# RWKV chunk stage of a two-layer mixer network: the inverse's second operand by transposes, a new block order, and merged right-hand sides

## The reference, cut to what matters

```python
def step(state, inp):
    w_t, kk_t, kka_t, k_t, v_t, r_t = inp
    sk = jnp.einsum('dbhvk,dbhk->dbhv', state, kk_t)
    new = (state * w_t[..., None, :] - sk[..., :, None] * kka_t[..., None, :]
           + v_t[..., :, None] * k_t[..., None, :])
    y_fwd = jnp.einsum('bhvk,bhk->bhv', new[0], r_t[0])
    y_bwd = jnp.einsum('bhvk,bhk->bhv', state[1], r_t[1])
    return new, jnp.stack([y_fwd, y_bwd])
```

## Time and profile before

| | |
|---|---|
| median of 3 runs | 3633.68 us (3628.63 to 3635.43) |
| profiled execution, its own time | 3633.06 us |
| its span, first to last instruction | 3631.3 us |
| PE busy | 3480.8 us (96%) |
| DVE, ACT, POOL busy | 1845.9, 1182.9, 667.7 us |
| stage of the change, layer 0 | 711.0 to 818.5 us |
| the same stage, layer 1 | 1916.2 to 2020.9 us |

### The profile page before, as it was taken

The page is one execution under the profiler, slowest core; times in us unless marked ns, Lnnn a source line. Parts: engine busy times, 40 slices in busy tenths (PEclk is TensorE's granted clock), DMA queues, the critical chain, the costliest instruction groups (busy, mean ns, idle before and its releaser), DMA issues. The chain is left out here.

```text
span 3631.3 us, 52208 instructions
## 1 busy us (share of the span) xinstructions
PE 3480.8 (96%) x22144; PEld 2769.1 (76%) x22144; DVE 1845.9 (51%) x2604; ACT 1182.9 (33%) x1641; POOL 667.7 (18%) x460
## 2 busy tenths in 40 slices
PE   7999998989999999999898899999899999989999
PEld 6888774586888788887548788887678887768887
DVE  6777636735455567664575543345543335373332
ACT  3222333524222322223352432233442223253223
POOL 4202111131202120211014121220011211001112
PEclk9999999999999999999999999999999999999999
DMA  6565421002444355442000222323032322122331
GB/s 210 179 195 171 129 72 35 7 27 83 124 148 125 113 166 188 152 155 82 31 13 27 71 89 92 101 83 93 24 105 93 101 96 85 59 70 93 96 101 58
DMA packets 445211, 357.99 MB, mean 99 GB/s; under 512 B 15990, under 2 KB 441012, under 8 KB 444980
## 3 DMA queue, kind: packets, MB, share of 16 engines
q1 hardware_dynamic: 444980, 354.67, 31.1%
HBM read 350.43 MB, written 2.10 MB: 97 GB/s over the span
## 5 line engine op out<-in xcount | busy, mean ns | idle before, releaser
L587 DVE TENSOR_TENSOR ring_wlo<-ring_raw,ring_whi 128x2048 fp32r<-128x2048 f32 (+3 forms) x268 | 570.9, 2130 | 376.6 <-ACT ring_whi L568 346.5
L568 ACT ACTIVATE ring_whi<-ring_raw 128x2048 fp32r<-128x2048 f32 (+3 forms) x278 | 490.4, 1765 | 652.0 <-PE f_ps L1076 242.9
L1074 PE MATMUL f_ps<-act_hi,ring_whi 128*128 128x512 f32 x1280 | 502.0, 392 | 3.3 <-DVEq L1228 3.3
L1076 PE MATMUL f_ps<-act_hi,ring_wlo 128*128 128x512 f32 x1280 | 498.7, 390 | 0.0
L1075 PE MATMUL f_ps<-act_lo,ring_whi 128*128 128x512 f32 x1280 | 498.1, 389 | 0.0
L1184 POOL TENSOR_TENSOR f_glo<-f_v,f_ghi 128x512 fp32r<-128x512 f32 x88 | 238.0, 2704 | 1030.2 <-ACT f_ghi L1176 1030.2
L1074 PEld LDWEIGHTS f_ps<-act_hi,ring_whi 128*128 128x128 f32 x1280 | 240.3, 188 | 53.6 <-DVEq L1228 5.0
L1166 ACT ACTIVATE f_t<-f_ps 128x512 f32<-128x512 f32 x88 | 52.6, 598 | 695.6 <-PE f_ps L1076 648.2
L1076 PEld LDWEIGHTS f_ps<-act_hi,ring_wlo 128*128 128x128 f32 x1280 | 240.2, 188 | 50.7
L1075 PEld LDWEIGHTS f_ps<-act_lo,ring_whi 128*128 128x128 f32 x1280 | 240.4, 188 | 49.0
L1074 PE MATMUL f_ps<-f_ghi,ring_whi 128*128 128x512 f32 x704 | 277.0, 393 | 0.0
(11 more groups left out here) (598 smaller groups left out, 6014.2 us busy)
## 6 DMA issues: line engine op xcount, KB each, us to landing
ring_raw<-in_w_ff_in SPq DMA_DIRECT2D x176, 512.0 KB, 4.8
f_ada_raw<-in_w_ada SPq DMA_DIRECT2D x128, 512.0 KB, 5.3
ring_raw<-in_w_mlp SPq DMA_DIRECT2D x64, 1024.0 KB, 5.1
ring_raw<-in_w_in SPq DMA_DIRECT2D x42, 1024.0 KB, 5.1
ring_raw<-in_w_ff_out SPq DMA_DIRECT2D x32, 768.0 KB, 4.5
ring_raw<-in_w_ff_out SPq DMA_DIRECT2D x32, 640.0 KB, 4.0
ring_raw<-in_w_out SPq DMA_DIRECT2D x16, 1024.0 KB, 5.5
ada_raw<-in_w_ada SPq DMA_DIRECT2D x16, 512.0 KB, 8.5
```

Source lines behind the costliest of these rows:

```text
L568: eng.activation(self.w_hi[:, i % self.SPLIT, 0:s.nk, 0:w], self.raw[:, i % self.RAW, 0:s.nk, 0:w], ACT.Copy)\
L587: eng.tensor_tensor(self.w_lo[:, i % self.SPLIT, 0:s.nk, 0:w], self.raw[:, i % self.RAW, 0:s.nk, 0:w], self.w_hi[:, i % self.SPLIT, 0:s.nk ...
L1074: eng.matmul(out, wh, o_hi[:, a, :], start=(s.first and q == 0), stop=False)
L1076: return eng.matmul(out, wl, o_hi[:, a, :], start=False, stop=(s.last and q == s.nk - 1))
```

## The change

It replaces the second half of the inverse's arithmetic by transposes, lays blocks half a level apart, and merges some operands.

- `mirrored` and its bank M are gone. `masked` (DVE, four operations on 64 partitions) writes the masked A part of MR into `MA`, with rows by head parity; `started` (DVE) makes the first T^T, tile `T1`, from the same bank; `kept` (DVE) masks the R part into `ME`. Only `kept` frees the banks of MR. POOL's four operations for T^T are gone.
- X is gone. After `second` has updated `T1`, `inverse_turned` (TN) transposes it with four 128x128 transposes and ACT copies the result into `T0`. `first` multiplies `MB` with `T0` on all four quarters of the array into two half-filled banks, each copied by ACT with its own operation.
- The negated BT lies beside the R part in `ME`, so `moved` is one matmul of 128 columns in place of two of 64. POOL sums the two directions of NR's second part (`summed`), so `ended` has three terms in place of four.
- Within a level PE does: Z(a), TN(a+1), other results, XT(a), Z(a+1), other results, TN(a), XT(a+1). The other results are placed anew; block 1's YQ, for which the weight loads wait, moves from the second to the fourth level of blocks 2 and 3. A third count "m" holds DVE's reads of MR, NR and RW.

```diff
@@ rwkv_chunks, tensor
-            def mirrored(b):
...
+            def inverse_turned(b, lv):
+
+                if lv == 0:
+                    eng.wait_ge(t_first, b + 1)
+                else:
+                    read(eng, "XT", b, lv)
+                out = begin("TN", b, lv)
+                for d in (0, 1):
+                    for hh in (0, 1):
+                        col = (2 * d + hh) * P
+                        mm = eng.transpose(out[:, col:col + P], T1[b][:, d, hh, :, :].rearrange("p q c -> p (q c)"), k.ident)
                 mm.then_inc(pe_done, 1)
...
             def first(b, lv):
                 i = b % 2
                 eng.wait_ge(mb_done, (b // 2 * LEVELS + lv - 1) * 2 + i + 1)
+                read(eng, "TN", b, lv - 1)
+                outs = [begin("Z", b, 2 * lv + par) for par in (0, 1)]
+                for d in (0, 1):
+                    for hh in (0, 1):
+                        col = (2 * d + hh) * 64
+                        for c in (0, 1):
+                            for par in (0, 1):
+                                mm = eng.matmul(outs[par][tok(c), col:col + 64], MB[i][tok(par), (lv + b // 2) % 2, d, hh, c, :],
+                                                T0[i][tok(par), d, hh, c, :], start=True, stop=True)
+                                if d and hh and c:
+                                    mm.then_inc(pe_done, 1)
...
-                if lv < LEVELS:
-                    out = begin("X", b, lv)
...
+            cross("MR", 0)
+            cross("MR", 1)
+            for name in ("AT", "BT", "KT"):
+                turned(name, 0)
+            inverse_turned(0, 0)
+            cross("NR", 0)
+            for a in (0, 2):
+                for lv in range(1, LEVELS + 1):
+                    first(a, lv)
+                    inverse_turned(a + 1, lv - 1)
+                    if a == 0 and lv in (1, 5):
+                        cross("NR", 1 if lv == 1 else 3)
+                    elif a == 0 and lv == 2:
+                        turned("AT", 1)
+                        turned("BT", 1)
+                    elif a == 0:
+                        cross("MR", lv - 1)
+                    elif lv == 1:
+                        solved(0)
+                    elif lv == 2:
+                        moved(0)
+                    elif lv < 5:
+                        ended(lv - 3)
+                    else:
+                        turned("AT", 3)
+                        turned("BT", 3)
+                    second(a, lv)
+                    first(a + 1, lv)
+                    if a == 0 and lv in (1, 3):
+                        guess(lv // 2)
+                    elif a == 0 and lv == 2:
+                        turned("KT", 1)
+                    elif a == 0 and lv == 4:
+                        cross("NR", 2)
+                    elif a == 2 and lv == 1:
+                        solved(1)
+                    elif a == 2 and lv == 2:
+                        moved(1)
+                    elif a == 2 and lv == 3:
+                        turned("AT", 2)
+                        turned("BT", 2)
+                    elif a == 2:
+                        turned("KT", lv - 2)
+                        guess(lv - 2)
+                    if lv < LEVELS:
+                        inverse_turned(a, lv)
+                    elif a == 0:
+                        inverse_turned(2, 0)
+                    second(a + 1, lv)
@@ vector
+            def masked(b):
+
                 for par in (0, 1):
+                    made(eng, "MR", b, par)
+                    for c in (0, 1):
+                        ins = eng.tensor_tensor(MA[b][tok(par), :, :, c, :], parts(bank("MR", b, par)[tok(c), :], 0),
+                                                k.unseen[tok(c), :, 0:64].unsqueeze(2).to_broadcast([64, 2, 2, 64]), ALU.mult)
+                ins.then_inc(a_masked, 1)
+
+            def started(b):
+
                 for par in (0, 1):
+                    ins = eng.tensor_tensor(T1[b][:, :, :, par, :], parts(bank("MR", b, par)[:, :], 0),
+                                            k.pairs.unsqueeze(2).to_broadcast([P, 2, 2, 64]), ALU.mult)
+                ins.then_inc(t_masked, 1)
+                eng.wait_ge(t_masked, b + 1)
+                t = T1[b][:, :, :, :, :].rearrange("p d h n c -> p (d h n) c")
                 eng.tensor_tensor(t, over_heads(k.eye64, 8), t, ALU.subtract).then_inc(t_first, 1)
 
+            def kept(b):
+
+                for par in (0, 1):
+                    eng.tensor_tensor(ME[b][:, :, :, par, 0, :], parts(bank("MR", b, par)[:, :], 1),
+                                      k.unseen[:, :, 64:P].unsqueeze(2).to_broadcast([P, 2, 2, 64]), ALU.mult).then_inc(m_read, 1)
...
             for b in (0, 1):
+                masked(b)
+                started(b)
+                kept(b)
+            later(0)
+            for a in (0, 2):
+                for lv in range(1, LEVELS + 1):
+                    if a == 0 and lv in (3, 4):
+                        masked(lv - 1)
+                    second(a, lv)
+                    if a == 0 and lv in (1, 5):
+                        later(1 if lv == 1 else 3)
+                    elif a == 0 and lv in (3, 4):
+                        started(lv - 1)
+                        kept(lv - 1)
+                    elif a == 2 and lv == 2:
+                        moved(0)
+                    second(a + 1, lv)
+                    if a == 0 and lv == 4:
+                        later(2)
...
```

More of the change, by code:

```diff
@@ L247, in _ @@
             for d in (0, 1):
-                added(k.pairs[:, d, :], k.between[:, 0, :], k.seen[:, 1 - d, 0:64], ALU.mult)
+                added(k.pairs[:, d, :], k.between[:, 0, :], k.seen[:, d, 0:64], ALU.mult)
             fill(k.eye64, 0.0)
@@ L2190, in cross, with one @@
     def cross(name, b):
[L2191 to L2200, removed]
+        order.extend([(name, b, 0, "m"), (name, b, 1, "m")])
+    def one(name, b, i=0):
+        order.append((name, b, i, "s"))
@@ L2209, in rwkv_plan @@
[L2209 to L2215, removed]
@@ L2222, in rwkv_plan @@
+    for b in (2, 3):
+        solved(b)
+    for b in (2, 3):
+        cross("RW", b)
+        ended(b)
+    place, reads = {}, {"v": 0, "s": 0, "m": 0}
     for n, (name, b, i, reader) in enumerate(order):
@@ L2296, in cross @@
                                     mm.then_inc(pe_done, 1)
-            def mirrored(b):
[L2299 to L2305, removed]
-                                mm = eng.matmul(outs[par][tok(c), col:col + 64], feat["A"][rows, 2 * d + hh, at:at + 64],
-                                                feat["B"][rows, 2 * d + hh, at:at + 64], start=True, stop=True)
-                                if d and hh and c:
-                                    mm.then_inc(pe_done, 1)
             def turned(name, b):
@@ L2446, in _ @@
-            for b in (0, 1):
-                solved(b)
-                mirrored(b + 2)
-            for lv in range(1, LEVELS + 1):
-                first(2, lv)
-                first(3, lv)
-                if lv <= 2:
-                    moved(lv - 1)
-                elif lv < LEVELS:
-                    turned("AT", lv - 1)
-                    turned("BT", lv - 1)
-                second(2, lv)
-                second(3, lv)
-                if lv <= 2:
-                    ended(lv - 1)
-                elif lv < LEVELS:
-                    turned("KT", lv - 1)
-                    guess(lv - 1)
@@ L2472, in _, with summed @@
             ph.clear(eng)
+            def summed(b):
+                read(eng, "NR", b, 1)
+                eng.tensor_tensor(NR[b][:, 0, :, 1, :], NR[b][:, 0, :, 1, :], NR[b][:, 1, :, 1, :], ALU.add).then_inc(n_summed, 1)
             for b in (0, 2):
@@ L2502, in _ @@
                         eng.tensor_tensor(z[:, t, 1:S + 1], z[:, t, 1:S + 1], z[:, 2 + t, 1:S + 1], ALU.mult).then_inc(rk_done, 1)
+                summed(b)
+                summed(b + 1)
         @block.scalar
@@ L2601, in moved @@
+            def second(b, lv):
+                made(eng, "XT", b, lv)
+                if lv > 1:
+                    read(eng, "XT", b, lv - 1)
+                else:
+                    eng.wait_ge(t_first, b + 1)
+                t = T1[b][:, :, :, :, :].rearrange("p d h n c -> p (d h n c)")
+                eng.tensor_tensor(t, t, bank("XT", b, lv)[:, :], ALU.subtract).then_inc(v_read, 1)
             def moved(b):
```

358 lines of the change are left out of this document (176 added, 182 removed).

## The result

The changed kernel takes 3607.45 us (median of 4 runs, 3604.77 to 3610.34). The kernel before took 3632.22 on the same chip (4 runs, 3628.63 to 3635.43). The ratio is 0.9932, 95% interval 0.9915 to 0.9949: faster, by 24.8 us, 0.7%. The forecast was 3610 from 3633.68. One run of experiment e3, of 5004.38 us, is left out of all that follows, since its mean granted clock was 0.65 where the other runs have 0.99, and nothing here says why.

A forecast was written before the change was run, and what follows sets the result against it. PE's own work bounds the stage; 92.0 of sets - 15.5 + 11.8 new waits + 6.3 code stops gives 94.6, so -12.9 in layer 0, -10.1 in layer 1, together -23.0: 3610 us from 3633.68, range 3594 to 3622.

The forecast's parts named there:

- The sets, -15.5 us a stage: PE's matmul sets in one stage: X, M go, Z faster, TN added, RW and YQ trimmed; together -15.5 us.
- The new waits, 11.8: PE waiting on DVE, ACT and banks, at the stage's start and in its levels: 11.8 us of new waits.
- The code stops, 6.3: PE stops for 256-instruction code blocks needing about 3.6 us, in `ended`, the tail and during weight loads: 6.3 us.
- Rival 1: Code stops in the stage vanish through fewer instructions and waits: 12.6 us less for two layers, 3597; chance 0.13.
- The sum, 94.6 a stage: Layer 0's stage after the change: 92.0 - 15.5 + 11.8 + 6.3 = 94.6 us, from 107.5.
- rival 2: Clock falls at the thin start in both layers for some 8 us, adding 4 us each: 3618; chance 0.14.
- a clock below 1 inside the stage: Sign that would show the prediction wrong: granted clock below 1 within the changed stage.
- Rival 3: DVE's queue binds and the waits double: both layers +23.6, no difference left, 3634; chance 0.08.
- rival 4: Thin start lowers the clock and level gaps keep it at 1.2 GHz: slower, 3656; chance 0.06.
- Rival 5: The chain of dependent operations is looser than reckoned, waits half: -12, 3598; chance 0.11.
- Costed at nothing: POOL's `summed`, ACT's added copies, SP's later weight loads (about 20 us left), and `pairs`: no time charged.
- The term of -9.2 us for Z: Z goes from two array quarters to four: 20 sets from 0.93 to 0.47 us, -9.2 us a stage.

The follow-up runs named there:

- e3: Changed kernel with DVE's subtraction from the identity moved behind `kept` for block 1 and behind block 1's XT subtraction for blocks 2 and 3: 3608.31 us, ratio 0.9941.
- the repetition: The changed kernel run and profiled once more, unaltered: 3609.31 us, ratio 0.9937 to the kernel before.
- e1: Changed kernel with `moved` issued as two matmuls of 64 columns in place of one of 128: 3618.07 us, ratio 0.9965.
- e2: Changed kernel with Z's same 16 matmuls ordered by head parity, so neighbours use only two quarters of the array: 3613.33 us, ratio 0.9956.
- e9: Kernel of e8 with Z's matmuls ordered by head parity as in e2: 3603.16 us, ratio 0.9917.
- e6: Changed kernel with the two blocks of a pair side by side again, not half a level apart: 3622.76 us, ratio 0.9972.
- e8: Changed kernel with 14 unused transposes filling the start, TN(a+1) after the other results, identity subtraction late (block 3's behind `later(2)`): 3598.81 us, ratio 0.9909.

## Why the prediction came out right

**The sets, -15.5 us a stage: right.** PE's busy time fell by 12.7 (with some 1 us of slow clock in it) and 14.3, in records whose ends overlap; TN 0.58, Z 0.47 and the 2496 matmuls are as reckoned.

**The new waits, 11.8: right in the sum.** 9.0 us of idle time before 12 sets in layer 0 and 9.4 before 13 in layer 1, with the estimated 0.2 of refilling each, make 11.4 and 12.0. By their terms: `t_first` 1.38 (1.3 reckoned); the banks behind `kept(1)` 3.09 (3.3); eight waits before TN of 0.29 + 0.2 (0.5); Z(0, 4) 0.54 (1.2); XT(1, 4) 1.64 (1.7). The wait of 0.5 in level 5 can't be told in the trace of layer 0, and the walk's 0.8 around the masks was not found as such.

**The code stops, 6.3: right in layer 0 of the first profile, too large elsewhere.** 5.7 and 3.6 us, with 0.8 of refills 6.5 and 4.4, and 3.7 and 2.5 in the repetition. e1 shows the cause as put: with 128 matmuls more there is more stopping, in layer 0 at new places, and again with the multiples of about 127 matmuls between the stops. The traces say it more sharply when PE's weight loads and semaphore instructions are counted too: between neighbouring stops of the changed kernel lie 513, 512 and 768 instructions in layer 0 and 511, 256 and 769 in layer 1. e2 and e9 are the other side of the same account: with sets that take longer the stops shrink, to 0.6 and 1.9 us in e2, from 3.9 and 4.9 to 2.2 and 3.5 in e9. The rule of the Trainium skill, page "Runtime: NRT & Kernel Launch", section "Instruction fetch mechanics", that the crossing of a block of 256 instructions is mostly hidden, holds while PE takes more than about 3.6 us for one. In this stage it doesn't hold: 127 matmuls and their loads that are done in 2.25 us were followed by the next only after 4.00. Rival 1, which rests on that rule, would have had the stages at 88, and stops of 3.6 to 5.7 us stand in the trace.

**The sum, 94.6 a stage.** Layer 0 came out at 96.9, layer 1 at 93.2. From the terms as measured: layer 0 is 76.5 of sets + 11.4 + 6.5 + 1.3 of clock = 95.7, with 1.2 left unexplained; layer 1 76.5 + 12.0 + 4.4 = 92.9. So 1.3 of the 2.3 us too many in layer 0 are rival 2 in small, and a clock below 1 inside the stage, which the prediction names as a sign of being wrong, did show. Rival 2's place was right: the clock falls to 1.2 GHz at the thin start. But its price was 4 us in both layers, and here it is 1.3 us in one: 3.4 us were slow, not 8, and during part of them PE waited anyway. And it isn't sure: the same 1.76 us of work in 4 us were followed by a fall in layer 0 and by none in layer 1. Over all profiles without filling it fell in 10 of 14 starts, for 3.4 or 6.8 us.

**Rival 3** (DVE's waits double) and **rival 4** (the clock stays low through the levels) did not happen. e1 and e6 come nearest to rival 4, with 7 to 17 us at 1.2 GHz in a stage; by 1.25 us for 3.4 slow that is up to 6 us a stage, so the mechanism exists and was far from spending the gain. **Rival 5** (a looser chain) didn't occur. e8 has its time, 3598.81 us where 3598 was reckoned, but not by its mechanism: there the waits went from 9 to 2.5 us by other orders and by filling, more than the half that rival 5 puts at 12 us for two stages, and 9 us came out. **Costed at nothing, and rightly:** the weights, issued at 788.11 in layer 0 and first used at 812.15 (ACT, L568), had 24 us where about 20 were reckoned.

**What was right by luck.** The term of -9.2 us for Z is a sum of set times, and it stands in the record as if all of it reached the end. It does not. e2 and e9 put Z back into a slower order and lose some 2 to 4 us a stage, where 4 to 7 us of PE's busy time were given up. The forecast held because the waits before TN and the code stops were in it as terms of their own. That they are the price of the faster Z, and go away with it, was not seen. Here the page "TensorEngine Tiling (Array Packing)" of the Trainium skill, section "PSUM Bottleneck", bears on it: it warns that packing speeds the matmuls up but not the reading of their results, which may then bind. In this trace the reading engines are not full (DVE 40 us of 93, ACT 41), so it isn't their throughput; but the wait before TN is the time from a result through DVE back to PE, and it appears when Z becomes short (some 0.3 us before TN in the changed kernel, none in e2).

The closeness of the two sums is luck as well. The layers were forecast to gain 12.9 and 10.1 us and gained 10.6 and 11.5, misses that partly cancel, and the same kernel's stage differs by 3.8 and 0.9 us from the first profile to the second.

**What stays open:** why the clock falls behind one thin stretch and not behind its twin. And no experiment puts X back in place of the transposes or takes the masks' new places apart, so what those parts are worth rests on the sets' times and the waits in the traces.

## What to carry to other kernels

When operations leave the bounding engine, count besides their time what had hidden behind them: here the handovers before TN and the fetching of code together took back half or more of what four-quarter matmuls saved, and each new wait costs some 0.2 us of refilling too (an estimate, from how far the records overlap). A wait that comes from an order in another engine's queue is only removed if the order behind it is mended as well: e3 alone gained nothing, and together with the mended order, the later TN and the filled start it was 9 us. Very dense stretches of small matmuls can be bound by their instructions, so fewer and wider ones (64x128 for two of 64x64) pay beyond their columns, as e1 shows.

## What the hardware showed beyond that

- PE stops at every 126 to 128 matmuls (with their loads), or a multiple of that, when they are done in less than about 3.6 us: 127 in 2.25 us, next only after 4.00. While 2 MB of weights arrive at about 300 GB/s a code block takes 6.3 to 7.3 us instead (126 matmuls, 5.55 us busy, in 6.63).
- Sixteen matmuls of 64x64 take 0.47 us when neighbours use different quarters, 0.77 to 0.87 when eight in a row take their rows from one half, and 0.93 in the kernel before.
- Short falls to the 1.2 GHz level happen inside a stage in which PE is busy for 85% of the time, 3.4 to 17 us of it in sum; 3.4 us of that cost 1.2 to 1.3, not 1.7; PE waited for a part of it (1.3 of e1's 6.8 us).
- At the thin start (in the changed kernel PE is busy there for 1.76 us of 4) the clock fell in 10 of 14 stages, and with 14 to 20 transposes put into the gap in none of 8. The filling alone gained nothing in the median.
- The same kernel's stage differs by up to 3.8 us from one execution to the next, mostly by the clock and the stops; its semaphore waits repeat to 0.1 us.
